# Where an expert's tokens come from: a table of rows in HBM in place of a selection product on TensorE

## The chip, the core and the metric

The program runs on one core of a Trainium2 chip. TensorE (PE) multiplies matrices, VectorE (DVE) and ScalarE (ACT) work on tiles, GpSimd (POOL) does small work and issues DMAs, SyncE (SP) issues DMAs. The metric is device microseconds (us) from start to end of one execution, the median of three runs.

## The reference

Two layers of a small encoder, in 32-bit floats, for 256 prompt tokens and 32 sample tokens (288 together), D_MODEL 1024. Each layer has a mixer of three recurrent or convolutional parts, cross-attention into 256 memory tokens, and a feed-forward part. The feed-forward part of layer 0 is dense (width 2816); that of layer 1 sends each token to the best two of eight experts:

```python
def swiglu(h, w1, w3, w2):
    return (jax.nn.silu(h @ w1) * (h @ w3)) @ w2

def moe(h, router, w1, w3, w2):
    logits = (h @ router).astype(jnp.float32)
    top_v, top_i = lax.top_k(logits, TOP_K)
    gates = jax.nn.softmax(top_v, axis=-1)
    dense_gate = jnp.sum(jax.nn.one_hot(top_i, N_EXPERTS, dtype=jnp.float32) * gates[..., None], axis=-2)
    out = jnp.zeros_like(h)
    for e in range(N_EXPERTS):
        out = out + dense_gate[..., e:e + 1].astype(h.dtype) * swiglu(h, w1[e], w3[e], w2[e])
    return out
```

A final RMSNorm follows, and the states, memory keys and values are outputs too.

## The kernel before

Each engine has an instruction stream of its own, written out by hand; they meet through semaphores. There is no planner: the order in the text is the order on the engine.

**Dense part (0 to about 880 us).** SP loads the weights of both layers in units of at most 1 MB into three slots of `ring`; a slot is loaded anew when TensorE has used its unit. The query and key columns of the mixer go to a tile of their own, `wqk`, in eight loads per layer with runs of 48 floats (L498). Results go through four PSUM banks, which ScalarE or VectorE empties in the order of `PLAN`.

**Expert part.** An expert's weights are 33 units of 1 MB, which SP loads into the 11 slots of `ring` (`load`, L520 to L532). For precision each unit is split: ScalarE writes the upper part `w_hi` (`weight_hi`), VectorE the rest `w_lo` (`weight_lo`, L2062), three places in turn, and each product is three. TensorE goes through 11 steps: `up(s)` multiplies the expert's tokens `hg_hi`, `hg_lo` (transposed, at most C=96 columns) by two units, ScalarE and VectorE form silu and product (`multiply`), `turn(s)` transposes that, ScalarE and VectorE split it again (`act_hi`, `act_lo`, L2073), and `down(s)` multiplies by a third unit. A `down` lags two steps, so that an expert ends with `turn(10)`, `down(9)`, `down(10)`. A loop runs experts 0 to 6, and the same text once more expert 7; further rounds follow where an expert has more than 96 tokens (`more`).

**Gather.** From the router's choice VectorE computes, for token and expert, the token's rank among the expert's tokens (`posr`, -1 and less where it isn't chosen). `sel` compares rank with 0 to 95. `gather(n)` (L1109) multiplies all 288 tokens `htok` by `sel`, three tiles for each of eight blocks of features, into PSUM banks 5 and 7: this gives the expert's tokens already transposed. Three more products give each rank's row number. ScalarE (`gather_hi`) and VectorE (`gather_lo`) make `hg_hi` and `hg_lo` of it. The gather for the next expert stands between the last step and `turn(10)`, and on VectorE `weight_lo` of unit 0 of the next expert comes ahead of `gather_lo`, and this ahead of `act_lo` of the last step.

**Outputs.** `copy_y` (L2056) takes the former expert's result out of PSUM at the start of the next. GpSimd sends its rows by an indirect DMA (L664) to `rows_y` in HBM, one row for each of a token's two choices, and then allows VectorE on (`y_free`, awaited at L2084, ahead of the next `sel`). In the last expert GpSimd reads first and second choices back (L671, L673), and VectorE adds them, times the gate, to the residual (`add_back`, L2117). Expert 7's own result is scattered by TensorE through a turned `sel`. `rows_y` was set to zero by one DMA on ScalarE's queue in layer 0 (L1403).

Of the kernel before, what the change touches and what calls it, by code (L numbers as in the profile page):

```python
# [33 lines left out]
NE = 8  # L34
# [80 lines left out]
def layer_program(nc, x_prompt, x_sample, state_gla, state_hgrn, state_rglru, state_conv, cache_mem_k, cache_mem_v,  # L115
# [7 lines left out]
    rows_y = nc.dram_tensor("moe_rows", [2 * T + C, D], F32, kind="Internal").ap()  # L123
    with ExitStack() as ctx:
# [47 lines left out]
        zrow = sb("zrow", [P, P])  # L172
# [42 lines left out]
        sil0 = view(low, 6912, 2, T)  # L215

# [5 lines left out]
        tok_no = view(low, 7552, 3, NE)  # L222
        row_no = view(low, 7576, 3, NE)
        id_col = view(low, 7600, 3)
        rs_tok = view(low, 7548, 3)
        lgT = view(low, 7256, T)
        spare_row = view(low, 7604, 1)
        row_at = view(low, 7606, 1).bitcast(U32)
        msq_y = view(low, 7608, 3)
        rs_y = view(low, 7612, 3)  # L230
        ids = view(low, 7616, 3, (MAXR + 1) * NE)
# [9 lines left out]
        iota_c = view(low, 9152, C)  # L241
        ytok = view(low, 0, 3, D)
# [121 lines left out]
        y_taken = sem("y_taken")  # L364
# [117 lines left out]
        def _(sp):  # L482
# [74 lines left out]
        def _(pool):  # L557
# [39 lines left out]
            for l in range(LAYERS):  # L597
# [36 lines left out]
                for g, (go, ho) in enumerate(((gla_p, hgrn_p), (gla_s, hgrn_s))):  # L634
                    for h in range(4):
# [10 lines left out]
            link(pool.iota(tok_no[:, :, :], [[P, 3], [0, NE]], base=-2 * T, channel_multiplier=1,  # L646
                           allow_small_or_imprecise_dtypes=True))
            link(pool.iota(spare_row[:, :], [[0, 1]], base=2 * T, channel_multiplier=1,
                           allow_small_or_imprecise_dtypes=True))
            link(pool.iota(row_at[:, :], [[0, 1]], base=2 * T, channel_multiplier=1))  # L650
            pool.sem_inc(const_ok, 1)
            pool.wait_ge(small_ready, 1)
# [5 lines left out]
            pool.wait_ge(rows_zeroed, 16)  # L658
# [20 lines left out]
        def _(pe):  # L679
# [427 lines left out]
            def gather(n):  # L1107

                pe.wait_ge(sel_ready, n)  # L1109
                for d in range(KD):  # L1110
                    out = ps[:, 5, C * d:C * d + C] if d < 5 else ps[:, 7, C * (d - 5):C * (d - 5) + C]
                    for t in range(3):
                        mm(out, htok[:, t, P * d:P * d + P], sel[:, t, :], t == 0, t == 2)
                for t in range(3):
                    last = mm(ps[0:C, 6, 0:1], sel[:, t, :], id_col[:, t:t + 1], t == 0, t == 2)
                last.then_inc(gathered, 1)

            gather(1)
# [8 lines left out]
            def expert(it, last_one):  # L1127
# [39 lines left out]
                if last_one:  # L1167
                    for t in range(3):
# [7 lines left out]
                if not last_one:  # L1176
                    gather(it + 2)
# [22 lines left out]
        def _(act):  # L1200
# [69 lines left out]
            for par_ in range(2):  # L1270
                act.dma_start(stage2[16:20, 64 * par_:64 * par_ + DK_G],
                               gla_ba.rearrange("l (g two k) -> (l g) two k", two=2, k=DK_G)[:, par_, :]
                               ).then_inc(params_in, 16)
            for l in range(LAYERS):
# [7 lines left out]
                for j in range(2):  # L1282
# [4 lines left out]
                    f(xc[:, j, 6 + TP:6 + TP + TS], ps[:, b, TP:T], ACT.Copy).then_inc(act_emptied, 1)  # L1287
                for j in range(2):
# [900 lines left out]
```

## Time and profile before

| | us |
|---|---|
| median of three runs (1723.6 to 1727.8) | 1727.54 |
| the profiled execution | 1722.73 |
| its span, first to last instruction | 1720.5 |
| TensorE busy, share of the span | 98% |
| VectorE, ScalarE, GpSimd | 64%, 54%, 6% |
| mean granted TensorE clock, share of full | 0.992 |

The span is cut by time into the dense part and the expert part; the profile calls engines PE, DVE, ACT, POOL and SP, and a line number after L is that of the kernel. Most TensorE instructions carry L683, a helper, so that they are told apart by their tiles: `ps<-low` with 128x96 is the gather (`htok` and `sel` lie in the tile `low`), `w_hi,hg_hi` is `up`, `w_hi,a_hi` is `down`. Weight loads of TensorE overlap products, and its busy time does not say how well it is used.

### The profile page before, as it was taken

Reading aid. Unit: us, or ns where it says so; the run is one execution under the profiler, and the core shown is the slowest. Engines: PE = TensorE matmul, PEld = TensorE weight load, DVE = VectorE, ACT = ScalarE, POOL = GpSimd, SP = SyncE. Lnnn points to the kernel's source line nnn. Section 1 sums busy time; section 2 is a strip of 40 time slices with the busy share of each in tenths; the row PEclk is TensorE's granted clock in tenths of the full one; section 3 lists DMA queues with packets and bytes.
Section 4 is the critical chain, followed back from the end, with each engine's and each line's share of the span. In section 5 each row is a group of like instructions: output and inputs, shape, how many; then the busy total and the mean of one; then the engine's idle time right before and its main releaser. Section 6 shows DMA issues by size and latency. Waiting matters only on the chain.

```text
span 1720.5 us, 32188 instructions
## 1 busy us (share of the span) xinstructions
PE 1689.9 (98%) x13385; PEld 1509.4 (88%) x13385; DVE 1109.5 (64%) x1236; ACT 930.3 (54%) x1071; POOL 101.8 (6%) x152
## 2 busy tenths in 40 slices
PE   7999999999999999999999999999999999999997
PEld 6788889999999777988888999999999999999996
DVE  5156516455544235623548888788888878888798
ACT  2334624444432133543357777676777767677675
POOL 3000210110001000101010000000000000000000
PEclk9999999999999999989999999999999999999999
DMA  8126363255457423426189999999999999999992
GB/s 216 56 76 197 106 193 132 80 173 171 155 146 186 104 74 106 164 56 224 63 294 325 365 317 374 317 369 366 323 366 324 374 316 369 367 325 366 322 365 89
DMA packets 356674, 400.60 MB, mean 233 GB/s; under 512 B 24892, under 2 KB 329688, under 8 KB 356584
## 3 DMA queue, kind: packets, MB, share of 16 engines
q1 hardware_dynamic: 345488, 381.58, 67.7%
q0 software_dynamic: 6176, 15.27, 2.5%
q10 hardware_dynamic: 4920, 2.43, 0.5%
q8 instruction: 71, 1.16, 0.3%
q14 instruction: 19, 0.16, 0.0%
HBM read 387.66 MB, written 11.58 MB: 232 GB/s over the span
## 4 chain that ended last, share of the span: by engine, by line
PE 95%; ACT 2%; DVE 2%; issue 1%; DMA 0%; DVEq 0%; SPq 0%; ACTq 0%
PE ps L683 93%; ACT ring L1218 1%; PE ps L1147 1%; PE ps L970 0%; ACT low L1218 0%; DMA ring<-in_x_sample_dram 0%; DVE dw_lo L1632 0%; DVE w_lo L2062 0%; PE ps L766 0%; ACT kvw_hi L1218 0%; PE ps L902 0%; DVE att L1934 0%; ACT L1218 0%; PE ps L844 0%; ACT rstd L1218 0%
## 5 line engine op out<-in xcount | busy, mean ns | idle before, releaser
L2062 DVE TENSOR_TENSOR w_lo<-ring,w_hi 128x2048 fp32r<-128x2048 f32 x264 | 604.1, 2291 | 101.3 <-ACT w_hi L1218 93.7
L1218 ACT ACTIVATE w_hi<-ring 128x2048 fp32r<-128x2048 f32 x264 | 504.5, 1914 | 126.9 <-PE ps L683 126.8
L683 PE MATMUL ps<-w_hi,hg_hi 128*96 128x256 f32 x1408 | 396.7, 282 | 2.3 <-DVE hg_lo L2051 2.3
L683 PE MATMUL ps<-w_hi,hg_lo 128*96 128x256 f32 x1408 | 395.2, 281 | 0.0
L683 PE MATMUL ps<-w_lo,hg_hi 128*96 128x256 f32 x1408 | 394.4, 280 | 0.0
L683 PEld LDWEIGHTS ps<-w_hi,hg_hi 128*96 128x96 f32 x1408 | 228.8, 162 | 7.3 <-issue 2.5
L683 PEld LDWEIGHTS ps<-w_lo,hg_hi 128*96 128x96 f32 x1408 | 227.9, 162 | 5.0
L683 PEld LDWEIGHTS ps<-w_hi,hg_lo 128*96 128x96 f32 x1408 | 229.3, 163 | 0.0
L1632 DVE TENSOR_TENSOR dw_lo<-ring,dw_hi 128x2048 fp32r<-128x2048 f32 (+1 forms) x54 | 113.1, 2094 | 106.5 <-ACT dw_hi L1218 106.5
L1218 ACT ACTIVATE low<-ps 96x256 f32<-96x256 f32 (+7 forms) x164 | 63.3, 393 | 186.9 <-PE ps L683 185.7
L1218 ACT ACTIVATE dw_hi<-ring 128x2048 fp32r<-128x2048 f32 (+1 forms) x54 | 94.6, 1753 | 109.7 <-PE ps L683 82.7
L683 PE MATMUL ps<-h_hi,dw_hi 128*128 128x288 f32 x480 | 143.4, 299 | 0.0
L683 PE MATMUL ps<-w_hi,a_hi 128*96 128x512 f32 x352 | 142.6, 405 | 0.0
L683 PE MATMUL ps<-h_hi,dw_lo 128*128 128x288 f32 x480 | 141.2, 294 | 0.0
L683 PE MATMUL ps<-w_hi,a_lo 128*96 128x512 f32 x352 | 138.5, 393 | 0.0
L683 PE MATMUL ps<-hT,ring 128*96 128x288 f32 (+2 forms) x544 | 134.9, 407 | 3.4 <-DVE hT L1661 3.4
L683 PE MATMUL ps<-w_lo,a_hi 128*96 128x512 f32 x352 | 138.1, 392 | 0.0
L683 PEld LDWEIGHTS ps<-hT,ring 128*96 128x96 f32 (+2 forms) x544 | 92.5, 172 | 42.7 <-issue 6.0
L683 PE MATMUL ps<-ffn_lo,dw_hi 128*128 128x288 f32 x352 | 103.8, 295 | 0.0
L683 PEld LDWEIGHTS ps<-h_hi,dw_lo 128*128 128x128 f32 x480 | 90.4, 188 | 0.0
L683 PEld LDWEIGHTS ps<-h_hi,dw_hi 128*128 128x128 f32 x480 | 90.0, 187 | 0.3
L683 PEld LDWEIGHTS ps<-w_hi,a_lo 128*96 128x96 f32 x352 | 56.7, 161 | 24.3
(310 smaller groups left out, 2675.6 us busy)
## 6 DMA issues: line engine op xcount, KB each, us to landing
ring<-in_moe_w_dram SPq DMA_DIRECT2D x264, 1024.0 KB, 6.9
ring<-in_ffd_w_dram SPq DMA_DIRECT2D x22, 1024.0 KB, 5.2
ring<-in_ffd_w_dram SPq DMA_DIRECT2D x16, 704.0 KB, 4.5
ring<-in_w_in_dram SPq DMA_DIRECT2D x14, 768.0 KB, 4.3
ring<-in_w_in_dram SPq DMA_DIRECT2D x8, 1024.0 KB, 5.7
ring<-in_xa_wk_dram SPq DMA_DIRECT2D x8, 1024.0 KB, 5.2
ring<-in_xa_wv_dram SPq DMA_DIRECT2D x8, 1024.0 KB, 6.0
ring<-in_xa_wq_dram SPq DMA_DIRECT2D x8, 1024.0 KB, 4.9
```

The costliest lines, as they stand in the source:

```text
L683: return nc.tensor.matmul(out, lhsT, rhs, start=first, stop=last)
L1147: last_ = nc.tensor.transpose(ps[:, 4, C * j:C * j + C], a_tok[0:C, s % 2, P * j:P * j + P], ident[0:C, 0:C])
L1218: return nc.scalar.activation(out, in_, func, **kw)
L1632: V.tensor_tensor(view(dw_lo, (n % DSLOTS) * SLOT, unit_words(n)), slot(n, unit_words(n)), view(hi_place(n, m), 0, unit_words(n)).bitcast( ...
L2062: V.tensor_tensor(view(w_lo, off, SLOT), view(ring, moe_slot(u) * SLOT, SLOT), view(w_hi, off, SLOT).bitcast(F32), ALU.subtract).then_inc( ...
```

## The change

Tokens are written once to a table in HBM, `rows_x`, at row 96*(1 + expert + 8*round) + rank in the round, by six indirect DMAs on GpSimd (two choices, three token tiles). Before each expert but the first, SP reads that expert's 96 rows into `x_rows` (over the first tile of `htok`), and TensorE turns them with eight transposes (`turn_rows`) in place of `gather`; the first expert keeps `gather`, without the row numbers. An expert's result is stored by a plain DMA to the same row numbers of `rows_y`, and read back by six indirect DMAs. Both tables now have 2400 rows and are set to zero, but for the first 96, by six DMAs on ScalarE's queue in layer 0. VectorE no longer makes `sel` and row numbers per expert; it makes the row table once ahead of the first expert, where its order changes too (`gather_lo(1)` ahead of `weight_lo(0, 1)`), and `sel` once more in the last expert.

```diff
+    rows_x = nc.dram_tensor("moe_in_rows", [(MAXR * NE + 1) * C, D], F32, kind="Internal").ap()
+    rows_y = nc.dram_tensor("moe_out_rows", [(MAXR * NE + 1) * C, D], F32, kind="Internal").ap()
...
+            sp.wait_ge(dispatched, 16 * 6)
             with sp.Fori(1, more * NE + NE) as it:
                 e = it & (NE - 1)
                 sp.lower_val(e)
+                row0 = it * C + C
+                sp.lower_val(row0)
+                sp.wait_ge(gathered, it)
+                sp.dma_start(x_rows[0:C, :], rows_x[bass.ds(row0, C), :]).then_inc(rows_in, 16)
                 for u in range(UNITS_E):
                     load(it, e, u)
...
+            pool.wait_ge(rows_zeroed, 16 * 2 * MAXR)
+            pool.wait_ge(htok_ready, 3)
+            pool.wait_ge(row_of_ready, 1)
+            for i in range(2):
+                for t, (t0, rows) in enumerate(TILES):
+                    pool.indirect_dma_start(rows_x[:, :], bass.IndirectOffsetOnAxis(ap=row_of[0:rows, i, t:t + 1], axis=0),
+                                            htok[0:rows, t, :], None).then_inc(dispatched, 16)
             pool.wait_ge(small_ready, 1)
...
             with pool.Fori(0, more * NE + NE) as it:
+                row0 = it * C
+                pool.lower_val(row0)
                 pool.wait_ge(y_scaled, it + 1)
-                pool.sem_inc(y_taken, 1)
-                pool.indirect_dma_start(rows_y[:, :], bass.IndirectOffsetOnAxis(ap=row_at[0:C, 0:1], axis=0),
-                                        y_sb[0:C, :], None).then_inc(y_put, 16)
+                pool.dma_start(rows_y[bass.ds(row0, C), :], y_sb[0:C, :]).then_inc(y_put, 16)
...
-                pool.dma_start(y_in[:, 0:2, :], rows_y[T * i:T * i + TP, :].rearrange("(t p) d -> p t d", p=P)
-                               ).then_inc(y_back, 16)
-                pool.dma_start(y_in[0:TS, 2, :], rows_y[T * i + TP:T * i + T, :]).then_inc(y_back, 16)
+                for t, (t0, rows) in enumerate(TILES):
+                    pool.indirect_dma_start(y_in[0:rows, t, :], None, rows_y[:, :],
+                                            bass.IndirectOffsetOnAxis(ap=row_of[0:rows, i, t:t + 1], axis=0)
+                                            ).then_inc(y_back, 16)
...
-                for t in range(3):
-                    last = mm(ps[0:C, 6, 0:1], sel[:, t, :], id_col[:, t:t + 1], t == 0, t == 2)
...
+            def turn_rows(n):
+                pe.wait_ge(rows_in, n * 16)
+                for d in range(KD):
+                    out = ps[:, 5, C * d:C * d + C] if d < 5 else ps[:, 7, C * (d - 5):C * (d - 5) + C]
+                    last_ = nc.tensor.transpose(out, x_rows[0:C, P * d:P * d + P], ident[0:C, 0:C])
+                last_.then_inc(gathered, 1)
...
                 if not last_one:
-                    gather(it + 2)
+                    turn_rows(it + 1)
...
+            def zero_rows(table, r):
+                n = NE * C
+                act.dma_start(table[C + r * n:C + r * n + n, :].rearrange("r d -> (r d)").rearrange(
+                                  "(p a n) -> p a n", p=P, n=2 * P),
+                              zrow.rearrange("p (a n) -> p a n", a=1).to_broadcast([P, n * D // (2 * P * P), 2 * P])
+                              ).then_inc(rows_zeroed, 16)
...
                     f(xc[:, j, 6 + TP:6 + TP + TS], ps[:, b, TP:T], ACT.Copy).then_inc(act_emptied, 1)
+                if l == 0:
+                    act.wait_ge(const_ok, 2)
+                    zero_rows(rows_x, 0)
...
+                    zero_rows(rows_x, 1)
...
+                    zero_rows(rows_x, 2)
 
                     act.wait_ge(mem_in, 16)
...
+                if last_one:
+                    for t in range(3):
+                        ins = V.tensor_scalar(sel[:, t, :], iota_c[:, :], posr[:, t, bass.ds(it, 1)], None, ALU.is_equal)
+                    ins.then_inc(sel_ready, 1)
                 copy_y(it)
...
                     dve.wait_ge(y_free, it + 1)
-                    V.tensor_scalar(row_at[0:C, :], ps[0:C, 6, 0:1], spare_row[0:C, 0:1], None, ALU.add)
-                    V.tensor_copy(id_col[:, :].rearrange("p (t e) -> p t e", e=1), ids[:, :, bass.ds(it + 1, 1)])
-                    for t in range(3):
-                        ins = V.tensor_scalar(sel[:, t, :], iota_c[:, :], posr[:, t, bass.ds(it + 1, 1)], None, ALU.is_equal)
-                    ins.then_inc(sel_ready, 1)
...
             weight_lo(0, 0)
+            link(V.tensor_tensor(row_tab[:, :, :], posr[:, :, 0:NE], row_base[:, :, :], ALU.add))
+            for r in range(1, MAXR):
+                link(V.tensor_scalar(gd[:, :, :], posr[:, :, 0:NE], float(C * r), float((NE - 1) * C), ALU.is_ge, ALU.mult))
+                link(V.tensor_tensor(row_tab[:, :, :], row_tab[:, :, :], gd[:, :, :], ALU.add))
+            for i, oh in enumerate((oh1, oh2)):
+                link(V.tensor_tensor(gd[:, :, :], row_tab[:, :, :], oh, ALU.mult))
+                link(V.tensor_reduce(row_f[:, i, :], gd[:, :, :], AX.X, ALU.add))
+            V.tensor_scalar(row_of[:, :, :], row_f[:, :, :], 0.0, None, ALU.add).then_inc(row_of_ready, 1)
+            gather_lo(1)
+            b = take("small")
+            V.tensor_copy(stage3[0:32, :], ps[0:32, b, 0:P]).then_inc(small_ready, 1)
             weight_lo(0, 1)
```

The three zeroings of `rows_y` stand in layer 0 too: in the place of the old one, behind the copies of the decayed keys, and behind the gate's silu.

## Rows read from the trace of the kernel before

**Rows 1.** The chain that ended last, whole run: shares of the span by engine.
```profile
PE 95%; ACT 2%; DVE 2%; issue 1%; DMA 0%; DVEq 0%; SPq 0%; ACTq 0%
```
**Rows 2.** Waits of TensorE, 905 to 1710 us: total us, times, longest us.
```profile
PE ps L683 <- DVE hg_lo L2051: 2.3, 1, 2.3
```
**Rows 3.** Timeline of TensorE at an expert boundary: start us, us, what, how often.
```profile
998.55 1.70 PE L683 MATMUL ps<-low 128*128 128x96 f32 x14
...
1004.34 0.36 PE L1147 MATMUL ps<-ident,low 96*128 96x96 f32 x2
...
1010.08 0.28 PE L683 MATMUL ps<-w_hi,hg_hi 128*96 128x256 f32 x1
```
**Rows 4.** Timeline of ScalarE at the same boundary; in brackets the idle time before.
```profile
998.75 1.91 ACT L1218 ACTIVATE w_hi<-ring 128x2048 fp32r<-128x2048 f32 x1 [0.54 <-PE ps L683]
```
**Rows 5.** Timeline of VectorE at the same boundary.
```profile
1000.70 2.29 DVE L2062 TENSOR_TENSOR w_lo<-ring,w_hi 128x2048 fp32r<-128x2048 f32 x1 [0.16 <-ACT w_hi L1218]
1005.42 0.66 DVE L2049 TENSOR_TENSOR hg_lo<-ps,hg_hi 128x480 fp32r<-128x480 f32 x1 [2.43 <-ACT hg_hi L1218]
...
1006.36 0.35 DVE L2073 TENSOR_TENSOR a_lo<-ps,a_hi 128x192 fp32r<-128x192 f32 x1
```
**Rows 6.** Timeline of GpSimd, first expert to last.
```profile
907.37 2.08 POOL L656 DMA_DIRECT2D out_dram<-low  x4 [17.86 <-DVE low L2139]
910.60 1.58 POOL L664 DMA_INDIRECT moe_rows<-low  x1 [1.16 <-issue]
...
1114.11 2.18 POOL L664 DMA_INDIRECT moe_rows<-low  x1 [98.21 <-DVE low L2056]
...
1664.58 0.74 POOL L671 DMA_DIRECT2D low<-moe_rows  x1 [39.34 <-DVE acc L2117]
```
**Rows 7.** Windows: us, busy PE PEld DVE ACT POOL, granted clock, DMA share, GB/s.
```profile
555.00:560.00 5.00, 2.49 (x9) 1.73 (x10) 2.67 (x7) 1.39 (x3) 2.42 (x2) 1.00 1.53 163
...
1010.00:1020.00 10.00, 10.00 (x87) 9.93 (x86) 8.74 (x6) 9.66 (x7) 2.19 (x1) 1.00 0.61 211
1020.00:1110.00 90.00, 90.00 (x652) 81.00 (x651) 75.55 (x59) 62.28 (x53) 0.00 (x0) 1.00 1.07 365
```
**Rows 8.** DMA issues, whole run: KB each, median us from issue to landing.
```profile
ring<-in_moe_w_dram SPq DMA_DIRECT2D x264, 1024.0 KB, 6.9
...
wqk<-in_w_in_dram SPq DMA_DIRECT2D x16, 192.0 KB, 5.9
moe_rows<-zrow ACTq DMA_DIRECT2D x1, 2304.0 KB, 16.6
...
moe_rows<-low POOLq DMA_INDIRECT x8, 7.1
```
**Rows 9.** Timelines of ScalarE, SP, TensorE, 25 to 35 us; the zeroing's issue.
```profile
25.94 0.47 ACT L1218 ACTIVATE ring<-ps 128x256 f32<-128x256 f32 x2 [3.36 <-PE ps L683]
...
26.32 2.51 SPq L498 DMA_DIRECT2D wqk<-in_w_in_dram  x1
...
33.50 15.68 PE L683 MATMUL ps<-hT,wqk 128*128 128x288 f32 x64
...
154.96 0.62 ACTq L1403 DMA_DIRECT2D moe_rows<-zrow  x1
```
**Rows 10.** Timeline of TensorE ahead of the first expert: transposes, and the first gather.
```profile
891.81 1.47 PE L817 MATMUL ps<-ident,xg 128*128 128x128 f32 x12
...
898.95 5.93 PE L683 MATMUL ps<-low 128*128 128x96 f32 x54
```
**Rows 11.** Timeline of VectorE in the first and in the last expert.
```profile
922.95 0.21 DVE L2085 TENSOR_SCALAR low<-ps,low 96x1 uint32<-96x1 f32 x1
...
1680.21 1.28 DVE L2117 SCALAR_TENSOR_TENSOR acc<-low,acc 128x1024 f32<-128x1024 f32 x1
```
**Rows 12.** The chain in order of time, first expert: start us, us, what.
```profile
927.20 2.89 PE ps L683 x13
```
**Rows 13.** The page's forty slices of 43 us: what the DMA engines moved.
```profile
GB/s 216 56 76 197 106 193 132 80 173 171 155 146 186 104 74 106 164 56 224 63 294 325 365 317 374 317 369 366 323 366 324 374 316 369 367 325 366 322 365 89
```

More of the change, by code:

```diff
@@ L215, in layer_program @@
         sil0 = view(low, 6912, 2, T)
+        zrow = view(low, 9536, 2 * P)
         htok = view(low, 0, 3, D)
@@ L221, in layer_program @@
         sel = view(low, 6968, 3, C)
-        tok_no = view(low, 7552, 3, NE)
-        row_no = view(low, 7576, 3, NE)
-        id_col = view(low, 7600, 3)
+        row_base = view(low, 7552, 3, NE)
+        row_tab = view(low, 7576, 3, NE)
         rs_tok = view(low, 7548, 3)
         lgT = view(low, 7256, T)
-        spare_row = view(low, 7604, 1)
-        row_at = view(low, 7606, 1).bitcast(U32)
         msq_y = view(low, 7608, 3)
         rs_y = view(low, 7612, 3)
-        ids = view(low, 7616, 3, (MAXR + 1) * NE)
+        row_f = view(low, 7616, 2, 3)
+        row_of = view(low, 7624, 2, 3).bitcast(U32)
         lgt = view(low, 7936, 3, NE)
@@ L241, in layer_program @@
         iota_c = view(low, 9152, C)
+        x_rows = view(low, 0, D)
         ytok = view(low, 0, 3, D)
@@ L363, in layer_program @@
         y_free = sem("y_free")
-        y_taken = sem("y_taken")
+        row_of_ready = sem("row_of_ready")
+        dispatched = sem("dispatched")
+        rows_in = sem("rows_in")
         y_back = sem("y_back")
@@ L1105, in _, with gather @@
             pe.wait_ge(htok_ready, 3)
-            def gather(n):
-                pe.wait_ge(sel_ready, n)
+            def gather():
+                pe.wait_ge(sel_ready, 1)
                 for d in range(KD):
@@ L1112, in gather @@
                     for t in range(3):
-                        mm(out, htok[:, t, P * d:P * d + P], sel[:, t, :], t == 0, t == 2)
-                for t in range(3):
-                    last = mm(ps[0:C, 6, 0:1], sel[:, t, :], id_col[:, t:t + 1], t == 0, t == 2)
-                last.then_inc(gathered, 1)
-            gather(1)
+                        last_ = mm(out, htok[:, t, P * d:P * d + P], sel[:, t, :], t == 0, t == 2)
+                last_.then_inc(gathered, 1)
[4 more added lines that the diff above has]
+                    last_ = nc.tensor.transpose(out, x_rows[0:C, P * d:P * d + P], ident[0:C, 0:C])
+                last_.then_inc(gathered, 1)
+            gather()
             pe.wait_ge(rounds_ready, 1)
@@ L1167, in expert @@
                 if last_one:
+                    pe.wait_ge(sel_ready, 2)
                     for t in range(3):
@@ L1401, in _ @@
                 if l == 0:
[L1402 to L1405 removed]
+                    zero_rows(rows_y, 0)
                 kv_copy(0, 5)
@@ L1410, in _ @@
                     f(kd_tok[0:rows, t, :], ps[0:rows, b, :], ACT.Copy).then_inc(act_emptied, 1)
+                if l == 0:
+                    zero_rows(rows_y, 1)
                 kv_copy(5, 5)
@@ L1422, in _ @@
                 kv_copy(10, 2)
+                if l == 0:
+                    zero_rows(rows_y, 2)
                 nc.scalar.preload_act_table_set("natural_log_exp_and_others")
@@ L2019, in _ @@
             dve.wait_ge(const_ok, 3)
-            link(V.scalar_tensor_tensor(out=row_no[:, :, :], in0=oh2, scalar=float(T), in1=tok_no[:, :, :],
-                                        op0=ALU.mult, op1=ALU.add))
             b = take("rank")
@@ L2026, in _ @@
             link(V.tensor_scalar(posr[:, :, 0:NE], tmp8[:, :, :], -1024.0, None, ALU.add))
-            V.tensor_tensor(id_col[:, :].rearrange("p (t e) -> p t e", e=1), row_no[:, :, 0:1], posr[:, :, 0:1], ALU.subtract)
             for t in range(3):
@@ L2113, in add_back @@
                 rows = TILES[t][1]
-                dve.wait_ge(y_back, 32 * (i + 1))
+                dve.wait_ge(y_back, 48 * (i + 1))
                 if i:
@@ L2123, in add_back @@
                         link(ins)
-            for r in range(MAXR + 1):
-                V.tensor_tensor(ids[:, :, NE * r:NE * r + NE], row_no[:, :, :], posr[:, :, NE * r:NE * r + NE], ALU.subtract)
             weight_lo(0, 0)
+            link(V.tensor_tensor(row_tab[:, :, :], posr[:, :, 0:NE], row_base[:, :, :], ALU.add))
[9 more added lines that the diff above has]
+            V.tensor_copy(stage3[0:32, :], ps[0:32, b, 0:P]).then_inc(small_ready, 1)
             weight_lo(0, 1)
@@ L2137, in _ @@
             link(V.tensor_tensor(gd[:, :, :], gd[:, :, :], tmp8[:, :, :], ALU.add))
-            b = take("small")
-            V.tensor_copy(stage3[0:32, :], ps[0:32, b, 0:P]).then_inc(small_ready, 1)
-            gather_lo(1)
             dve.wait_ge(act_emptied, emptied("xt", 5))
```

13 lines of the change are left out of this document (2 added, 11 removed).

## The prediction

> **What bounds the kernel now.** I read the chain of waits first: TensorE holds 95% of it [rows 1]. The waits of TensorE from the first expert to the end come next: one entry of note, 2.3 us before the first expert, none inside the expert loop [rows 2]. So in the loop an instruction taken off TensorE shortens the time, until another engine is late. Then the PE timeline of one expert boundary [rows 3], with ScalarE and VectorE over the same stretch [rows 4, 5], to see what would be late. The scatter on GpSimd came 98.21 us after the former one ended, which itself took 2.18: an expert takes 100.4 us [rows 6]. Last the DMA load in and between boundaries [rows 7, 8], and the first stage [rows 9].
>
> **The gather, seven times.** The gather starts at 998.55 and the transposes behind it at 1004.34: 5.79 us [rows 3]. That is 54 passes (24 products and 3 for the row numbers, two passes each), as the first gather shows: 54 in 5.93 us [rows 10]. Afterwards eight transposes of 96x128 stand there. Twelve 128x128 transposes took 1.47 us, 0.12 each [rows 10], so eight cost 0.96. Gross 4.83 us for each of the seven boundaries.
>
> Not all of it comes back, because the gather covers the splitting of the next weights. Let T0 be the gather's start, 998.55. ScalarE's w_hi at 998.75 is unit 0 of the next expert: it waits for the last product before the gather and ends at T0+2.1 [rows 4]. VectorE splits that unit from 1000.70 for 2.29, to T0+4.4 [rows 5]. Only then come hg_lo and a_lo of the last step; from 1005.42 to the end of a_lo, 1006.36+0.35, is 1.3 us [rows 5]. These two do not wait for more: hg_hi can run at T0+2.1, when the transposes are done. So a_lo ends at about T0+5.75, and the last `down` waits for it. TensorE gets there at T0+0.96, plus 0.2 for turn(10), plus one `down`; from 1004.34 to 1010.08 there are a turn and two of them, 5.74, so one is 2.77. That is T0+3.9. It will stand 1.85 us, waiting for a_lo. The boundary lasts 5.8+2.77=8.6 instead of 11.53. Gain 2.95 us, times seven: -20.7. Ends: 4.83 each (-33.8), if the stall were hidden, and 0, if the rows came late. I take the middle value, because each term has its own row.
>
> A pause of that size should not change the clock: in the 5 us from 555 TensorE worked only 2.49 and the granted clock stayed at 1.00, the 2.4 GHz level [rows 7].
>
> **The DMA of x_rows.** SP issues it behind unit 32 of the former expert, which waits for the split of unit 21 of 33. About ten units remain until the turn; at some 2.8 us each, as the `down` above, that is 28 us. A weight load lands in 6.9 us [rows 8]. Cost zero; if the cover is gone, TensorE waits up to 6.9 per expert, and turn(10) behind it. Ahead of it SP has new waits, for the six scatters (over by about 930, see below) and for the former turn (an expert earlier); all later loads are queued behind them, and SP comes there after both. Its 0.39 MB add 1.1 us of transfer at 365 GB/s, the rate in the stretch 1020 to 1110; at the boundary the DMA is only 0.61 busy and 211 GB/s [rows 7]. Per expert then 34.6+0.39+0.39=35.4 MB, 97.0 us at 365, against the new period of 97.4. It just fits, and the ring of 11 units (31 us, less 6.9 for landing) is some 24 us ahead.
>
> The Trainium skill, "DMA: Bandwidth & Descriptors", Specifications, speaks against this change: it gives an HBM limit of about 358 GB/s per core. By that the period could not fall under 35.4/0.358=98.9 us and the gain would be 1.5 per expert, -10.5 in all. The trace shows 365 GB/s over 90 us, so I go by the trace.
>
> **VectorE and the y store in the loop.** VectorE loses row_at, id_col and three selection rows per expert (0.21 for the first [rows 11]); it is not the bound between boundaries, so nothing. The store of y becomes plain; as an indirect one it landed in 7.1 [rows 8], and in the first expert 12.3 us lie between its issue at 910.60 [rows 6] and VectorE's next instruction behind the wait, at 922.95 [rows 11]. Nothing; ends 0 and +1 each.
>
> **Before the first expert.** Three row-number products less, 0.66 (six passes of 0.11 [rows 10]), and hg_lo is moved ahead of the second w_lo, so that the 2.3 us wait [rows 2] shrinks: -0.9, ends 0 and -2. But GpSimd now issues six indirect scatters there. It was released at 907.4 for the four small stores [rows 6]; the row table adds about four small VectorE operations of 0.2, and one w_lo of 2.29 now stands behind it, so the scatters start near 905.5. Each takes 1.58 to 2.18 to issue [rows 6]: 9.5 to 13.1. Then the four stores, 2.08, and the load of the loop count, 1.2: the first y store is issued at 918.3 to 921.9 instead of 910.6. It lands 7 us later, behind 2.36 MB of scattered rows: 925 to 929. VectorE stops at the wait for y_free, which stood at 922.95 with no delay [rows 11]. Queued behind it are unit 6's w_lo (2.29) and a_lo (0.35), and TensorE's first `down`, which began about 927.2 [rows 12], needs both. With y free at 927.5 TensorE starts that `down` at 930.1, and it would have started about 926.3: +4, ends 0 and +8.
>
> **The zeroing in layer 0.** Six DMAs of 3.1 MB replace one of 2.36 MB: 16.5 MB more. The old one took 16.6 us beside weight loads [rows 8]. Five of the six fall where slack is at hand or little else moves. The first does not: it is issued after the rx copies, at 26.4 [rows 9]. The last of eight wqk loads is issued from 26.32 to 28.83 [rows 9] and lands 5.9 later [rows 8], at 32.2; TensorE starts on wqk at 33.50 [rows 9], 1.3 us later. These loads are of 192-byte rows and share the engines with 1 KB writes. Below, they are not slowed: 0. Above, the whole zero DMA comes first, 3.1 MB at 365 GB/s is 8.6, less 1.3: +7. I take +4, since the old zero DMA of 2.36 MB, 6.5 us at that rate, needed 16.6 in company [rows 8], a sharing by more than half.
>
> The Trainium skill, same page, Queues, rings and completion order, says that an engine goes round its queues packet by packet; by that small rows lose most beside large ones, and the stall is near its upper end and the sum, an estimate, -9.7; no row of the trace shows such loads beside such writes.
>
> An issue on ScalarE costs 0.62 [rows 9]; the one ahead of the memory norm is on the chain there: +0.4. The key and value projections: +0.5 (0 to +4), since their units are loaded one or two ahead.
>
> **The last expert.** Reading back is three indirect DMAs per pass. The second set is issued at 1664.6 [rows 6] and first used at 1680.2 [rows 11]; three issues of 2.18 and a landing of 7.1 make 13.6 of 15.6. Nothing; ends 0 and +4. The three selection rows come back here before copy_y, three times 0.21 on VectorE [rows 11]: 0 to +0.6, I take 0, and TensorE's wait for them falls two `up` later.
>
> **Sum.** -20.7 -0.9 +4 +4 +0.4 +0.5 = -12.7. The profiled execution took 1722.7 (span 1720.5): it becomes 1710. The median of the three runs shown, 1727.5, is 4.8 above that execution, the lowest run 0.9 above; from the median it would be 1714.8. I say 1712.
>
> **Rivals.**
> *All the added traffic hides.* Both +4 go to zero, -21.6: 1701 to 1706. For: the second and third slices of the page moved only 56 and 76 GB/s [rows 13]. Against: 1.3 us before wqk, and GpSimd's queue before the first y.
> *The DMA sets the period.* Over 1010 to 1110 the mean is 350 GB/s, between boundaries 365 [rows 7]. If the core gets no more than the middle, 357, then 35.4 MB take 99.1 us: 1.3 per expert, -9 instead of -20.7, 1722 to 1727. For: the loads run at that level for 90 of 100 us, with the added rows as new traffic. Against: the lead of the ring. The page on DMA named above puts its limit there too.
> *The boundary only changes its wait.* a_lo, or rows_in, arrives as late as the gather ended: -20.7 falls to about 0 and the sum is +8: 1731 to 1735. For: hg_lo waits for ScalarE in the trace too [rows 5]. Against: that wait is for the gather itself.
> *Slower: the zeroing starves the dense stage.* 16.5 MB at 365 GB/s are 45 us of DMA time while weights have three slots. If more than about 17 us of it (the -21.6 less the first expert's +4) shows as TensorE waits in layer 0, the kernel is slower than before; with half of it, 22.6 us, 1727.5-17.6+22.6=1732. For: the old zero DMA took 16.6 for 6.5 us of transfer [rows 8], so it and the loads held each other up. Against: seven of the first eight slices moved under 200 GB/s [rows 13].
>
> **How the numbers follow.** Chances: forecast 0.48, all hidden 0.17, DMA period 0.10, wait changes place 0.10, slower 0.15. About 0.3% (5 us) is what a measurement of this kernel can tell from no change. Faster: 0.48+0.17, and 0.06 of the DMA case (where it takes less than that), 0.71. Slower: 0.12 of the last and 0.04 of the one whose wait changes place, 0.16. Same: what is left of these three, 0.13. The range goes from the hidden case, less 4 us for a smaller boundary stall, to the starved case: 1697 to 1732; the forecast's own is 1703 to 1721.
>
> **What would show it.** Seven PE waits near 1.9 us on a_lo, one before each last `down`; period 97.4; eight transposes of 1 us where the gather was; no PE wait for x_rows. One wait of some 4 us in the first expert, with VectorE held for the y store. A wait for wqk near 33 us. The forecast is wrong if the period is over 99 or under 96, or if layer 0 grows by more than 10 us.

## The result and the profile after

The kernel became slower, by 0.45%. It took 1732.68 us (median of 20 executions, 1729.53 to 1737.71), the kernel before 1725.16 (20 executions, 1719.27 to 1731.65): ratio 1.0045, 95% interval 1.0035 to 1.0055, or +7.5 us. The prediction was 1712, with 1697 to 1732 as its range, and -12.7 us as the change. The profiled execution took 1729.59, its span is 1727.8, 7.3 us above that of before.

**The expert loop.** The page of the changed kernel, the chain that ended last:

```profile
PE 91%; ACT 3%; DVE 2%; issue 2%; DMA 1%; POOL 1%; DVEq 0%; POOLq 0%; SPq 0%; ACTq 0%
```

TensorE has gone from 95% of the chain [rows 1] to 91%, so it now waits for others more often. Its waits, 905 to 1710 us (total, times, longest), where there was one entry of 2.3 [rows 2]:

```profile
PE ps L694 <- DVE a_lo L2102: 14.0, 7, 2.0
PE ps L1164 <- DVE a_lo L2102: 2.8, 1, 2.8
PE ps L694 <- DVE low L2164: 2.3, 1, 2.3
```

The timeline of TensorE (start us, us, what, how often; in brackets the idle time before): two points of layer 0, one of the first expert, and the first two boundaries:

```profile
21.27 15.76 PE L694 MATMUL ps<-hT,ring 128*128 128x288 f32 x64 [1.71 <-DVE hT L1693]
...
198.12 5.35 PE L694 MATMUL ps<-ring,low 128*96 128x128 f32 x24 [3.78 <-issue]
...
943.75 0.55 PE L1164 MATMUL ps<-ident,low 96*128 96x96 f32 x2 [2.78 <-DVE a_lo L2102]
...
1016.87 0.83 PE L1132 MATMUL ps<-ident,low 96*128 96x96 f32 x8
...
1022.64 0.47 PE L694 MATMUL ps<-w_hi,a_hi 128*96 128x512 f32 x1 [2.00 <-DVE a_lo L2102]
...
1114.31 0.83 PE L1132 MATMUL ps<-ident,low 96*128 96x96 f32 x8
...
1120.08 0.47 PE L694 MATMUL ps<-w_hi,a_hi 128*96 128x512 f32 x1 [2.00 <-DVE a_lo L2102]
...
1121.24 0.63 PE L694 MATMUL ps<-w_lo,a_hi 128*96 128x512 f32 x1
```

The boundary is as predicted up to this: eight transposes in 0.83 us where 5.79 stood [rows 3], and a wait of 2.00 (1.85 was forecast). The first boundary, 1016.87 to the next expert's first product at 1025.49, is 8.6 us, as forecast, against 11.53 in [rows 3]. The second, 1114.31 to 1124.49, is 10.2: the products behind its wait take 0.63 us each instead of 0.39. Windows of the same kernel (us, five engines' busy time, granted clock, DMA share, GB/s) say why:

```profile
198.00:200.00 2.00, 1.88 (x11) 1.45 (x12) 0.00 (x0) 1.97 (x3) 0.55 (x2) 0.82 0.21 55
200.00:212.00 12.00, 12.00 (x98) 11.19 (x99) 4.21 (x5) 7.58 (x13) 0.00 (x0) 0.50 0.80 264
...
1030.00:1120.00 90.00, 88.08 (x642) 79.42 (x640) 78.43 (x55) 67.47 (x57) 0.00 (x0) 1.00 1.08 360
...
1118.00:1120.00 2.00, 0.08 (x1) 0.00 (x0) 1.95 (x4) 1.89 (x1) 0.00 (x0) 1.00 1.10 358
1120.00:1122.00 2.00, 1.92 (x6) 1.38 (x7) 1.95 (x1) 0.02 (x1) 0.00 (x0) 0.72 1.06 392
1122.00:1124.00 2.00, 2.00 (x6) 1.32 (x5) 0.35 (x1) 0.00 (x0) 0.00 (x0) 0.50 1.04 371
```

Behind the pause the granted clock is at 0.50, the 1.2 GHz level. That comes after six of the seven boundaries, not after the first. GpSimd's stores of y give the period, and the first expert's late one:

```profile
926.17 3.31 POOL L661 DMA_INDIRECT moe_in_rows<-low  x1 [0.30 <-issue]
...
935.05 0.54 POOL L675 DMA_DIRECT2D moe_out_rows<-low  x1
...
1126.58 0.51 POOL L675 DMA_DIRECT2D moe_out_rows<-low  x1 [98.45 <-DVE low L2085]
1225.57 0.51 POOL L675 DMA_DIRECT2D moe_out_rows<-low  x1 [98.48 <-DVE low L2085]
```

The period is 98.99 us, against 100.40 [rows 6]: 1.4 gained per expert, where 2.95 was forecast. VectorE, first expert and second boundary:

```profile
941.04 2.29 DVE L2091 TENSOR_TENSOR w_lo<-ring,w_hi 128x2048 fp32r<-128x2048 f32 x1 [4.07 <-POOLq L677]
...
1116.46 2.29 DVE L2091 TENSOR_TENSOR w_lo<-ring,w_hi 128x2048 fp32r<-128x2048 f32 x1 [0.16 <-ACT w_hi L1236]
1118.67 0.65 DVE L2078 TENSOR_TENSOR hg_lo<-ps,hg_hi 128x480 fp32r<-128x480 f32 x1
...
1119.60 0.35 DVE L2102 TENSOR_TENSOR a_lo<-ps,a_hi 128x192 fp32r<-128x192 f32 x1
```

The next expert's w_lo and hg_lo still stand ahead of the last a_lo, as in [rows 5]; what was hidden by the gather is now TensorE's wait.

**Layer 0.** TensorE stood 3.78 us at 198 and then worked twelve us at 0.50; before, the same products began at 190.49 and no low clock followed. ScalarE just ahead of that:

```profile
175.58 1.92 ACT L1236 ACTIVATE kvw_hi<-ring 128x2048 fp32r<-128x2048 f32 x1 [3.37 <-DMA ring<-in_xa_wv_dram]
...
182.95 1.92 ACT L1236 ACTIVATE kvw_hi<-ring 128x2048 fp32r<-128x2048 f32 x1 [2.38 <-DMA ring<-in_xa_wv_dram]
...
192.17 1.92 ACT L1236 ACTIVATE kvw_hi<-ring 128x2048 fp32r<-128x2048 f32 x1 [4.55 <-DMA ring<-in_xa_wv_dram]
194.00 4.03 ACT L1236 ACTIVATE ring<-low 32x128 f32<-32x128 f32 x18
```

ScalarE waits three times for the value weights, 10.3 us in all (0.6 before), and behind the third split stand the eighteen copies (`a_full`). In the program TensorE waits for them; they end at 198.03 and it starts at 198.12. The DMA issues (KB each, median us to landing) show the zeroings of `rows_y` (`moe_out_rows`) and the value weights, which took 6.0 before:

```profile
moe_out_rows<-low ACTq DMA_DIRECT2D x3, 3072.0 KB, 17.7
...
ring<-in_xa_wv_dram SPq DMA_DIRECT2D x8, 1024.0 KB, 7.1
```

Point by point through the two profiled executions, the changed kernel less the one before: first products of layer 0 +3.4 (21.27 against 17.91, the sum of squares ahead of them took 7.0 instead of 4.2 in the same code); memory transposes +3.7; start of the mixer's output products +16.1 (of the 12.4 since the transposes, 3.8 are the stall and 8.4 the slower products behind it); layer 1 +14.2 (the kernel before lost some 2 us at 304 to 308 to a low clock that this execution lacks); first gather +14.4; start of the first boundary +18.3; then the boundaries, -3.0 and six times -1.4, and +0.4 at the end: +7.3.

### The profile page after: what moved, and what is told of

Read it like the earlier page. It is cut to its first block, busy times and chain, and to the rows that moved or that the text cites. A ratio compares the mean times of both kernels' runs of the same rounds, so it can differ in the third digit from the quotient of the medians.

```text
span 1727.8 us, 31528 instructions
## 1 busy us (share of the span) xinstructions
PE 1676.5 (97%) x13057; PEld 1488.1 (86%) x13057; DVE 1107.8 (64%) x1208; ACT 929.1 (54%) x1071; POOL 110.3 (6%) x158
## 4 chain that ended last, share of the span: by engine, by line
PE 91%; ACT 3%; DVE 2%; issue 2%; DMA 1%; POOL 1%; DVEq 0%; POOLq 0%; SPq 0%; ACTq 0%
PE ps L694 89%; ACT ring L1236 1%; PE ps L1164 1%; ACT w_hi L1236 1%; POOL moe_in_rows L661 0%; PE ps L981 0%; DMA moe_out_rows<-low 0%; DMA ring<-in_x_sample_dram 0%; ACT low L1236 0%; PE ps L777 0%; DVE dw_lo L1664 0%; DVE hg_lo L2078 0%; ACT kvw_hi L1236 0%; DVE w_lo L2091 0%; PE ps L913 0%
## 5 line engine op out<-in xcount | busy, mean ns | idle before, releaser
L694 PE MATMUL ps<-w_hi,a_hi 128*96 128x512 f32 x352 | 148.0, 420 | 14.0 <-DVE a_lo L2102 14.0
L694 PE MATMUL ps<-w_lo,a_hi 128*96 128x512 f32 x352 | 142.8, 406 | 0.0
L694 PE MATMUL ps<-w_hi,a_lo 128*96 128x512 f32 x352 | 142.3, 404 | 0.0
L694 PEld LDWEIGHTS ps<-w_hi,a_hi 128*96 128x96 f32 x352 | 58.8, 167 | 36.8 <-issue 17.3
```

The source lines that it names most:

```text
L694: return nc.tensor.matmul(out, lhsT, rhs, start=first, stop=last)
```

## The experiments

Every experiment is named by its ratio to the kernel before, run beside it; differences to the changed kernel are taken from its 1.0045, one ratio point of 0.001 being 1.7 us. The intervals of the ratios are some 2 to 4 us to either side, so a difference of two is good to 3 or 4 us.

**1. Zeroing of rows_y moved out of the key and value stage.**

```diff
-                if l == 0:
-                    zero_rows(rows_y, 0)
                 kv_copy(0, 5)
...
+                    zero_rows(rows_y, 0)

                 act.wait_ge(ri_ready, l + 1)
...
+                else:
+                    zero_rows(rows_y, 1)
```

The first now stands behind the copies of the memory transposes in layer 0, the second behind the rx copies and the third behind the q copies of layer 1.

> The changed kernel with the three zeroings of rows_y moved, bytes unchanged: one behind the memory transposes of layer 0, two behind the rx and q copies of layer 1. Theory: these zeroings made the key and value weights late, ScalarE's queue with them, and TensorE stood 3.8 us and then worked at a granted clock of 0.50 for most of 198 to 228. Then this wait and this clock go, the span from the first hT product to the start of the out products falls by about 12 us, and the time is about 1720.5 (ratio to before 0.9975). Rival 1, the bytes cost wherever they stand: the same 12 us come back as TensorE waits in layer 1's mixer or near the memory part, 1732. Rival 2, that stage was slow in one profiled execution only: no change of the median, 1732, and the wait is absent or present at random.

Measured: 1721.0 us, ratio 0.999 (0.9972 to 1.0008), -9.5 us. TensorE's timeline in this kernel has the stage's products without a wait:

```profile
192.94 3.54 PE L694 MATMUL ps<-ring,low 128*96 128x128 f32 x24
```

and ScalarE waits for no value weights. Of the 12 us that the stall and the clock behind it took in the profile of the changed kernel, 9.5 came back with the same bytes elsewhere: what was paid is mainly the place, not the volume.

**2. TensorE kept busy in the boundary's pause.**

```diff
                 down(STEPS - 2)
+                if not last_one:
+                    for _ in range(16):
+                        nc.tensor.transpose(ps[:, 6, 0:P], ident[:, :], ident[:, :])
                 down(STEPS - 1)
```

> The changed kernel with sixteen 128x128 transposes of the identity, about 1.9 us, into an unused bank of PSUM between down(9) and down(10) of experts 0 to 6, where TensorE stood 2.0 us; no work of use is added. Theory: the pause lowers the granted clock to 0.50 behind six of the seven boundaries, which costs 1.6 us each. With TensorE busy in the pause the clock stays at 1.00, the period falls from 98.99 to about 97.4, the time by about 9.6 to 1723 (ratio 0.999). Rival 1, the clock falls for another cause (the changed operations, a rise of power with DMA): period 99.0, 1732. Rival 2, the DMA sets the period: the clock stays at 1.00, but TensorE waits for weights instead, period 99.0, 1732.

Measured: 1724.17 us, ratio 0.9992 (0.9978 to 1.0007), -9.1 us. TensorE, second boundary, then GpSimd:

```profile
1122.65 1.91 PE L1200 MATMUL ps<-ident 128*128 128x128 f32 x16
1124.81 0.47 PE L694 MATMUL ps<-w_hi,a_hi 128*96 128x512 f32 x1 [0.25 <-DVE a_lo L2105]
```

```profile
925.43 8.04 POOL L661 DMA_INDIRECT moe_in_rows<-low  x1 [0.30 <-issue]
...
1129.74 0.51 POOL L675 DMA_DIRECT2D moe_out_rows<-low  x1 [96.89 <-DVE low L2088]
1227.16 0.51 POOL L675 DMA_DIRECT2D moe_out_rows<-low  x1 [96.91 <-DVE low L2088]
```

The window in which the clock fell before (same columns as above):

```profile
1122.00:1124.00 2.00, 2.00 (x17) 1.77 (x16) 2.00 (x3) 1.29 (x2) 0.00 (x0) 1.00 1.11 360
```

Sixteen useless transposes make the period 97.42, the forecast's 97.4, and the clock stays at 1.00. So the pause itself cost what was forecast and the clock behind it the rest. This also ends a rival that looked proven: the period of 98.99 is within 0.1 of the 98.9 that follows from the limit of about 358 GB/s which the Trainium skill, "DMA: Bandwidth & Descriptors", Specifications, gives. The loads were not what set it. The same run shows a miss of the forecast: one scatter's issue took 8.04 us where it had taken 3.31, and the first expert's wait was 8.8 us, not 2.8.

**3. Another order at the boundary.**

```diff
                     weight_hi(it + 1, 0)
-                    gather_hi(it + 2)
                 act_hi(STEPS - 1)
                 if not last_one:
+                    gather_hi(it + 2)
...
-                if not last_one:
-                    weight_lo(it + 1, 0)
-                    gather_lo(it + 2)
                 act_lo(STEPS - 1)
                 if not last_one:
-                    for u in range(1, SPLITS - 1):
+                    gather_lo(it + 2)
+                    for u in range(SPLITS - 1):
                         weight_lo(it + 1, u)
```

> The changed kernel with another order at the boundary: on ScalarE act_hi of the last step ahead of gather_hi, on VectorE act_lo of the last step and gather_lo ahead of weight_lo of the next expert's unit 0. Theory: a_lo ends about 4.2 us before it did, the 2.0 us wait of TensorE goes and with it the fall of the clock; the next unit 0 is split at 6.5 us after the boundary's start, just before TensorE wants it at 6.7. Period 98.99-2.0-1.6=95.4, seven times -3.6, time 1707.5 (ratio 0.990). Rival 1, DMA: 35.4 MB per expert at 365 GB/s are 97.0 us, so the period stops there, TensorE waits for weights, 1718 (ratio 0.996). Rival 2, the wait changes its place: TensorE stands the same 2 us at the next expert's first product for hg_lo or w_lo, 1732.

Measured: 1716.4 us, ratio 0.9955 (0.9939 to 0.9972), -15.5 us. VectorE at the second boundary:

```profile
1120.13 0.36 DVE L2102 TENSOR_TENSOR a_lo<-ps,a_hi 128x192 fp32r<-128x192 f32 x1 [0.38 <-ACT a_hi L1236]
1120.89 0.66 DVE L2078 TENSOR_TENSOR hg_lo<-ps,hg_hi 128x480 fp32r<-128x480 f32 x1 [0.41 <-ACT hg_hi L1236]
...
1121.83 4.48 DVE L2091 TENSOR_TENSOR w_lo<-ring,w_hi 128x2048 fp32r<-128x2048 f32 x2
```

No wait is left there, no fall of the clock, and the period is 95.3 as the theory said (stores at 1128.11 and 1223.41). The median falls short of the theory's -25 by ten us. In the profile the loop gives nearly all of it, 21.6 between the stores of the second and the last expert (572.3 for 593.9) and 2.0 at the first boundary; but the first expert waited 8.9 instead of 2.8, the q and k products waited 2.8 for wqk, and the last expert was 2.6 us longer, with 2.7 of new waits for w_lo. The median of -15.5 lies near the DMA rival's number, not its mechanism, which asked for a period of 97.0 in every expert.

**4. The first store of y ahead of the scatters.**

```diff
+            pool.wait_ge(y_scaled, 1)
+            pool.dma_start(rows_y[0:C, :], y_sb[0:C, :]).then_inc(y_put, 16)
+            pool.wait_ge(y_put, 16)
+            pool.sem_inc(y_free, 1)
             for i in range(2):
...
-            with pool.Fori(0, more * NE + NE) as it:
+            with pool.Fori(1, more * NE + NE) as it:
```

> The changed kernel with GpSimd's first store of y (expert loop's turn 0) and its y_free ahead of the six scatters and four small stores instead of behind them. Theory: VectorE's wait of 4.07 us for y_free in the first expert goes, TensorE's 2.8 us for a_lo behind it, and part of the low clock of 942 to 948: about -5, 1727.7 (ratio 1.0015). Rival 1, the store would land late anyway because the DMA rings are full there: the wait stays, 1732. Rival 2, slower: the scatters, now 20 us later, hold up the loads behind them on SP: TensorE waits at the start of the second expert, over 1735.

Measured: 1729.01 us, ratio 1.0026 (1.0011 to 1.0041), -3.3 us with an uncertainty of some 3, so this gain is hardly shown. TensorE's wait for a_lo in the first expert is gone; this profiled execution has instead a wait of 4.3 us for wqk.

**5. The three edits together.** No diff beyond those of 1, 3 and 4.

> The moved zeroings of rows_y, the other order at the boundary and the early first store together. Measured alone, against the changed kernel's 1.0045 times before, they gave about -9.5 us, -15.5 us and -3.3 us. Theory: three places in time that don't touch each other, so the gains add: -28, 1704 (ratio to before 0.988); the order's own run had 8.9 us of waiting in the first expert, which the early store takes away, so somewhat more is possible, 1698. Rival, DMA: at a period of 95.3 the loads need 371 GB/s, the most seen; with the first expert earlier the ring has less lead and the waits for weights in the last experts eat 5 to 8 us, 1710.

Measured: 1707.65 us, ratio 0.9903 (0.9889 to 0.9918), -24.5 us, between the theory's 1704 and the rival's 1710. Two things show. The stores of y stand 95.1 to 95.3 apart for four experts and then 97.25 and 98.5; experiments 6 and 10 show what sets the last periods. And TensorE:

```profile
38.26 18.69 PE L698 MATMUL ps<-hT,wqk 128*128 128x288 f32 x64 [4.62 <-DMA wqk<-in_w_in_dram]
```

It waited 4.6 us for wqk, and 64 products took 18.7 instead of 15.7 [rows 9], with the granted clock at 0.50 from 40 to 44. In the expert loop the loads got 361 to 362 GB/s per expert, not the 371 that the expectation names.

**6. The zeroing of rows_x moved too.** In `zero_rows` calls alone: none ahead of the q and k products, one each behind the q copies, the memory transposes and two gate copies; the three of rows_y are all in layer 1.

> As the run with all three edits, and the zeroings of rows_x moved too: none before the q and k products, so that none is in flight beside the loads of wqk; the first behind the q copies, one behind the memory transposes, one behind two gate copies; those of rows_y behind the rx and q copies and two gate copies of layer 1. Theory: the wait for wqk (2.8 and 4.3 us in two profiled executions, hidden in three others whose start was 2 to 3 us later) and the low clock behind it go in all executions: -2 to -5 against the run with three edits, 1700 (ratio 0.986). Rival: that wait is filled by the late start in most executions, so 0; or the zeroings beside the gates bring the waits back there, +4.

Measured: 1701.11 us, ratio 0.9859 (0.984 to 0.9877): -32 us against the changed kernel, -24 against the one before, the fastest version. Its start was a quick one, and wqk is waited for no more; TensorE:

```profile
33.65 15.68 PE L698 MATMUL ps<-hT,wqk 128*128 128x288 f32 x64
```

GpSimd's stores, ScalarE's waits for weights, 1000 to 1700 us, and two windows, in the same kernel:

```profile
1297.73 0.51 POOL L679 DMA_DIRECT2D moe_out_rows<-low  x1 [94.79 <-DVE low L2086]
1394.75 0.51 POOL L679 DMA_DIRECT2D moe_out_rows<-low  x1 [96.52 <-DVE low L2086]
1492.36 0.51 POOL L679 DMA_DIRECT2D moe_out_rows<-low  x1 [97.11 <-DVE low L2086]
```

```profile
ACT w_hi L1240 <- DMA ring<-in_moe_w_dram: 41.1, 35, 2.8
```

```profile
1030.00:1120.00 90.00, 90.00 (x658) 81.44 (x657) 79.17 (x55) 67.62 (x56) 0.51 (x1) 1.00 1.08 361
...
1300.00:1390.00 90.00, 89.18 (x639) 79.52 (x637) 76.94 (x55) 65.81 (x56) 0.00 (x0) 1.00 1.07 361
```

The changed kernel itself had no such ScalarE entry. The DMA moves 361 GB/s in the early experts as in the late ones, though 35.4 MB in 95.3 us would be 371. So the early experts use about 1 MB more each than arrives meanwhile, out of the weights that lie ready in the ring; from 1300 on, ScalarE waits for loads.

**7. The zeroings alone, on the kernel before.**

```diff
+    spare_y = nc.dram_tensor("spare_rows", [2 * NE * C, D], F32, kind="Internal").ap()
...
+                if l == 0:
+                    act.dma_start(spare_y[0 * NE * C:0 * NE * C + NE * C, :].rearrange("r d -> (r d)").rearrange(
...
+                                  ).then_inc(rows_zeroed, 16)
```

The zeroing stands twice, with 3.1 MB each, where the changed kernel has its second and third of rows_y.

> The kernel before, with nothing of the change but two more zeroings of 3.1 MB of a spare table, in the places where the changed kernel has its second and third for rows_y (its own 2.36 MB stay at the first). Theory: the key and value stage stalls as in the changed kernel, TensorE stands 2 to 4 us and works at the low clock behind it: +10, 1735 (ratio 1.006). Rival: without the other parts of the change there is no stall, 1725 (ratio 1.000), and the stall of the changed kernel comes from more than the bytes in this place.

Measured: 1731.7 us, ratio 1.0046 (1.0033 to 1.006), +8 us. TensorE, then ScalarE's wait, 150 to 230 us:

```profile
193.50 5.21 PE L684 MATMUL ps<-ring,low 128*96 128x128 f32 x24 [2.92 <-issue]
```

```profile
ACT kvw_hi L1219 <- DMA ring<-in_xa_wv_dram: 4.3, 2, 3.7
```

The stall and the low clock (0.50, 196 to 208) appear with nothing else of the change. Put in, they cost 8; taken out in experiment 1, 9.5.

**8. The first zeroing of rows_x later.**

```diff
                     act.wait_ge(const_ok, 2)
-                    zero_rows(rows_x, 0)
...
+                    zero_rows(rows_x, 0)
                     zero_rows(rows_x, 1)
```

> The changed kernel with the first zeroing of rows_x issued behind the q copies, together with the second, instead of behind the rx copies, where it runs beside the loads of wqk. Theory: the wait for wqk goes where the start is quick: profile without it and q and k products from 33.5 or, after a slow start, 35 to 37; on the median -2 (0 to -4.5), 1730.5 (ratio 1.003). Rival, as the prediction had it: a full +4 in every execution, so -4 or more, 1728 (ratio 1.0015).

Measured: 1737.76 us, ratio 1.0085 (1.0067 to 1.0103), +7 us: both theories wrong. ScalarE and its queue:

```profile
43.41 5.82 ACTq L1294 DMA_DIRECT2D moe_in_rows<-low  x2
...
51.17 7.15 ACTq L1294 DMA_DIRECT2D moe_in_rows<-low  x1
```

and TensorE:

```profile
66.34 3.68 PE L855 MATMUL ps<-ident,ring 128*128 128x128 f32 x16 [7.45 <-ACTq L1338]
```

With three zeroings close together, an issue that took 0.55 us alone takes 5.8 for two and 7.15 for the third. ScalarE does nothing meanwhile, the memory norm comes late, and TensorE stands 7.45 us. The start of this execution was late as well, so it does not speak on wqk.

**9. The two failed steps repaired, nothing else.** The diffs of 1 and 2.

> The changed kernel with the two repairs that priced the failed steps of the prediction, and nothing else: the zeroings of rows_y moved (alone -9.5 us) and the transposes that keep TensorE busy in the boundary's pause (alone -9.1 us). The 2.0 us of the pause itself, the wait for y_free in the first expert and the wait for wqk stay, as the prediction had them. Theory, these two steps are all that failed: 1732.7-18.6=1714, ratio 0.9935, about the predicted 1712 to 1715. Rival, a further loss is hidden behind them (loads that set the period once it is 97.4, as in the last experts of the run with three edits): the period grows in the last experts, 1720, ratio 0.997.

Measured: 1713.01 us, ratio 0.9943 (0.9925 to 0.996), -17.6 us. Periods are 97.4 from the second expert to the last, so no further limit hides at that period. Times the 1725.16 of before, this is 1715.3.

**10. More bytes in the fastest version.**

```diff
-                pool.wait_ge(y_put, it * 16 + 16)
+                pool.dma_start(spare_y[:, :], y_sb[0:C, :]).then_inc(y_put, 16)
+                pool.wait_ge(y_put, it * 32 + 16)
```

> The fastest version (three edits and the zeroings of rows_x moved; 0.9859 of before) with every store of y from the second expert on made twice, the second copy into a spare table: 0.39 MB more per expert, nothing else. In that version the period is 95.3 for three experts and 97.0 to 98.5 for the last ones, at 359 to 368 GB/s. Theory: there the DMA sets the period, the ring's lead being used up; 7 x 0.39 MB at 361 GB/s are 7.6 us, and all of it shows: 1709 (ratio 0.990), the long periods near 99 and from an expert earlier. Rival: the long periods come from ScalarE or VectorE, the bytes hide beside them: 1701 to 1702 (ratio 0.986).

Measured: 1709.88 us, ratio 0.9928 (0.9904 to 0.9952), +12 with an uncertainty of some 5, against 7.6 forecast. GpSimd's stores, then ScalarE's waits:

```profile
1393.74 0.51 POOL L680 DMA_DIRECT2D moe_out_rows<-low  x1 [98.27 <-DVE low L2088]
...
1492.98 0.51 POOL L680 DMA_DIRECT2D moe_out_rows<-low  x1 [98.24 <-DVE low L2088]
```

```profile
ACT w_hi L1242 <- DMA ring<-in_moe_w_dram: 99.4, 114, 3.6
```

ScalarE's waits for weights more than double. VectorE has to wait for both stores here, but the trace has no such wait between 1000 and 1700, so the bytes are what costs. In the late experts of versions 5, 6 and 10 the DMA sets the period: 35.8 MB in 99.24 us here are 361 GB/s. That lies near the 358 of the limit that the Trainium skill, "DMA: Bandwidth & Descriptors", Specifications, gives. It is no sharp one: the kernel before moved 365 over 90 us [rows 7]. That it is not felt in the first experts fits the ring's lead, by the windows of experiment 6; a longer or shorter ring was not tried.

## Why the prediction was wrong

**The step that failed first: "A pause of that size should not change the clock."** It rested on the 5 us of [rows 7] with TensorE busy for half the time at 1.00. That row shows one place, and the same trace has the opposite. Behind the 2.3 us that TensorE waits ahead of the first expert [rows 2], a wait of the forecast size, the kernel before ran like this:

```profile
908.00:910.00 2.00, 1.86 (x10) 1.87 (x10) 2.00 (x3) 0.24 (x1) 1.45 (x3) 0.59 0.91 229
```

Its products took 0.41 us there and 0.28 from 912 on, and it has more low-clock stretches (734 to 742, 846 to 850). So one row was taken for the rule. The pause had the forecast length, 2.00 for 1.85, but 1.6 us per boundary went to the clock behind it, at six of seven. Experiment 2 gives 9.1 us for it, and its period of 97.42 is the forecast's. So the term -20.7 was right as a count of waits and lacked +9. The sign set for this, a period over 99, was too loose: 98.99 lies just inside it with half of the gain gone.

**The second: key and value projections "+0.5 (0 to +4), since their units are loaded one or two ahead".** It was 8 (put in, experiment 7) to 9.5 (taken out, experiment 1); "Five of the six fall where slack is at hand or little else moves" is the same step. The working asked whether TensorE's weights come late, by the distance of the loads, and not what stands behind a late split on ScalarE's own stream: the `a_full` copies, due at that moment. TensorE's stand of 3.8 us is less than half of it; the clock behind it is the rest in the profile. The sign set for this, layer 0 longer by more than 10 us, came true: layer 1 began 14.2 late, 10.8 without the slow start.

Together 9.1 and 9.0 (9.5 less the 0.5 counted) are 18, good to some 5 us. The miss against the median forecast, 1714.8, is 17.9, and experiment 9 with both repaired comes to 1715.3. So close a match is in part luck: 1714.8 starts from a median of three, 1727.5, where twenty executions gave 1725.16. As a change, -12.7 was forecast and +7.5 came, 20.2 apart; experiment 9 gives -9.8 (-12.9 to -6.9), so some 3 us can lie in the other terms.

**The other terms.** Gross transposes: 0.96 forecast, 0.83 measured. *Wait in the first expert, +4*: TensorE waited 2.8 in this execution and in experiment 1, and 8.8 to 9.0 in four others (2, 3, 8, 9), where the fourth scatter's issue took 8.0; the early store gained 3.3. The place was right; four of six executions lie above the stated end of +8. *The smaller wait before the first expert, -0.9*: the wait stayed at 2.3, 1.6 in some other runs; the gather lost its six passes. *wqk, +4 (0 to +7)*: right, but only in some executions. Where TensorE starts at 18 us, it waited 2.8, 4.3, 4.6 and 2.9 (experiments 3, 4, 5, 9); where it starts at 20 to 21 (the profiled one, 1, 2), the loads landed in time. Moving the zeroings (experiment 6 against 5) gave 7.6 us with an uncertainty of 4; in 5's profile, the slowest of its five executions, the wait of 4.6 and the slower products behind it, 18.7 for 15.7, make the same, and the low clock at 204 to 220 some 4 more. The rule of the Trainium skill, "DMA: Bandwidth & Descriptors", Queues, rings and completion order, that an engine goes round its queues packet by packet, put the wait near +7; the trace has 2.8 to 4.6 beside a zeroing and none without, so it agrees in kind and not in size. *Memory norm, +0.4*: +0.35. *x_rows, last expert*: in the changed kernel nothing waits for them. The -21.6 of the first rival leaves out +0.4 and +0.5 as well; with them it is -20.7.

**The rivals.** "The DMA sets the period" was wrong here, though its period was met: the loop ran 97.4 and 95.3 without one byte less. It comes true at a period of 95.3, after three or four experts, when the ring's lead is used up: 35.4 MB at 361 GB/s are 98.1 us (an estimate from experiment 6), so a much longer loop would not keep even 97.4. "Zeroing starves the dense stage" was right in kind and 8 to 9.5 us in size, half of the 17 it needed by itself. "The boundary only changes its wait" was right in half of its amount, through the clock and not through a later a_lo. No rival had two half losses together, and an upper end of only +4 on the projections kept the range from it.

**What stays open.** Why the first sums of squares take 4.15 us in some executions and 5.7 to 7.0 in others, at a recorded clock of 1.00. Why one scatter's issue takes 3.3 or 8.0 us. And why, in experiments 5 and 9, the clock fell at 202 to 222 with no wait there at all: the low clock of that stage is not the stall's alone. Both profiled executions were the slowest of theirs (1722.66 of 1707 to 1723 in experiment 9), and two of the twelve of experiment 1 took 1730 and 1732, so this can be most of that spread, which is not shown.

## What to carry to other kernels

When an operation is taken off the bounding engine, cost what it covered, and then cost the clock behind the hole, from every wait of that size in the trace and not from one: move the late operation ahead (a_lo before the next expert's weights, -3.6 us per boundary) before counting the gain. Price a background DMA in the stage where it runs, by what waits on the issuing engine's own stream and which loads it meets, not by its bytes over the mean rate. When a period agrees with a limit, change something else and see whether it moves before believing it.

## What the runs showed of the hardware

- A pause of 2.0 us in work that is otherwise continuous left TensorE at half clock for some 3 us, after six of seven boundaries here and after all seven in experiments 1, 4 and 8; sixteen transposes in its place kept the clock at 1.00.
- Issuing a 3.1 MB DMA on ScalarE's queue took 0.55 us by itself; with three close together (experiment 8) two took 5.8 and the third 7.15, and ScalarE did nothing else meanwhile.
- The six indirect scatters took 0.85 to 8.04 us each to issue on GpSimd.
- The DMA moved 360 to 363 GB/s per expert in experiments 3, 6 and 10, at periods of 95 to 100 us alike.
